# Input products of the mixers in another order, with attention and statistics woven between them

## The reference

```python
u = x @ w_in
u_conv, u_lru, q, k, v = jnp.split(u, [o1, o2, o3, o4], axis=-1)
y_conv = _conv_module(u_conv, conv_dw_w, conv_dw_b, conv_ln_g, conv_ln_b)
y_lru = _recurrent(u_lru, lru_conv_w, lru_conv_b, lru_wa, lru_ba, lru_wx, lru_bx, lru_lambda)
y_attn = _swa(q, k, v, band_bias, valid, sinks)
return jnp.concatenate([y_conv, y_lru, y_attn], axis=-1) @ w_out
```

## Time and profile before

| | |
|---|---|
| median of 3 runs | 3671.16 us (3669.0 to 3671.75) |
| the profiled execution | 3668.6 us, its span 3666.9 us |
| TensorE busy | 3374.3 us (92% of the span) |
| VectorE, ScalarE, GpSimd busy | 1614.5, 653.2, 310.9 us |
| stretch of mixer 0, first product to first output product | 465.4 to 652.2 us of the span |
| the same in mixer 1 | 1582.7 to 1772.2 us |

### The profile page before, as it was taken

The page is one execution under the profiler, slowest core; times in us unless marked ns, Lnnn a source line. Parts: engine busy times, 40 slices in busy tenths (PEclk is TensorE's granted clock), DMA queues, the critical chain, the costliest instruction groups (busy, mean ns, idle before and its releaser), DMA issues. The chain is left out here.

```text
span 3666.9 us, 38396 instructions
## 1 busy us (share of the span) xinstructions
PE 3374.3 (92%) x14592; PEld 2311.5 (63%) x14592; DVE 1614.5 (44%) x2304; ACT 653.2 (18%) x1051; POOL 310.9 (8%) x240
## 2 busy tenths in 40 slices
PE   6999995899998999986889998899969999899998
PEld 5888842488887888843478886745844443434342
DVE  4665355366636665446266644434334001311112
ACT  1111014211101111013221101422543000100001
POOL 2110000111101111000111101000320000100000
PEclk8999997999999999997999998899989999899999
DMA  5442220334323343221224421222112232799996
GB/s 135 108 124 80 80 62 19 81 86 114 95 89 87 91 114 94 80 58 35 81 66 106 109 86 48 69 69 81 35 45 71 72 100 93 306 409 410 410 407 240
DMA packets 490114, 453.18 MB, mean 124 GB/s; under 512 B 33994, under 2 KB 438781, under 8 KB 489756
## 3 DMA queue, kind: packets, MB, share of 16 engines
q1 hardware_dynamic: 487920, 449.97, 38.6%
q10 hardware_dynamic: 1452, 1.67, 0.4%
q0 software_dynamic: 640, 0.15, 0.0%
HBM read 445.96 MB, written 5.77 MB: 123 GB/s over the span
## 5 line engine op out<-in xcount | busy, mean ns | idle before, releaser
L454 PE MATMUL psum<-arena 128*128 128x256 f32 x7392 | 1621.6, 381 | 20.3 <-DVE arena L782 20.3
L454 PEld LDWEIGHTS psum<-arena 128*128 128x128 f32 x7392 | 1403.1, 190 | 221.4 <-issue 23.2
L847 DVE TENSOR_TENSOR arena<-arena 128x512 f32<-128x512 f32 (+2 forms) x152 | 96.5, 635 | 607.8 <-PE psum L454 578.8
L2118 PE MATMUL psum<-arena 128*64 128x512 f32 x1536 | 344.3, 598 | 0.8 <-ACT arena L2227 0.8
L351 POOL TENSOR_TENSOR arena<-arena 128x1024 f32<-128x1024 f32 x96 | 180.8, 1906 | 1045.8 <-DVE arena L837 1001.3
L2118 PEld LDWEIGHTS psum<-arena 128*64 128x64 f32 x1536 | 105.8, 136 | 231.9 <-issue 231.0
L678 ACT COPY arena<-psum 128x256 f32<-128x256 f32 x104 | 38.9, 374 | 1182.8 <-PE psum L454 1182.8
L1355 PE MATMUL psum<-arena 128*128 128x512 f32 (+1 forms) x576 | 216.8, 537 | 12.8 <-ACT arena L1571 6.5
L1547 PE MATMUL psum<-arena 128*128 128x512 f32 x512 | 220.3, 591 | 0.0
L2334 DVE SCALAR_TENSOR_TENSOR arena<-psum,arena 128x512 f32<-128x512 f32 x64 | 48.0, 751 | 330.4 <-PE psum L2128 330.1
L562 PE MATMUL psum<-arena 128*128 128x512 f32 x416 | 184.0, 603 | 9.8 <-DVE arena L991 6.3
(11 more groups left out here) (393 smaller groups left out, 2911.6 us busy)
## 6 DMA issues: line engine op xcount, KB each, us to landing
arena<-in_w_gate_dram SPq DMA_DIRECT2D x64, 1024.0 KB, 14.1
arena<-in_w_up_dram SPq DMA_DIRECT2D x64, 1024.0 KB, 14.6
arena<-in_w_down_dram SPq DMA_DIRECT2D x64, 1024.0 KB, 16.9
arena<-in_ffn_w_gate_dram SPq DMA_DIRECT2D x88, 512.0 KB, 5.6
arena<-in_ffn_w_up_dram SPq DMA_DIRECT2D x88, 512.0 KB, 7.2
arena<-in_ffn_w_down_dram SPq DMA_DIRECT2D x96, 384.0 KB, 3.8
arena<-in_w_in_dram SPq DMA_DIRECT2D x144, 256.0 KB, 3.2
arena<-in_ada_w_dram SPq DMA_DIRECT2D x48, 512.0 KB, 4.0
```

Of the source, the lines that this page charges most:

```text
L454: mm = pe.matmul(psum[:, b0 + b, c:c + HT], w, right(x), start=(first and c == 0), stop=last, skip_group_check=True)
L847: dve.tensor_tensor(sv[:, 0, :, :], a21, a22, ALU.add)
L2118: mm = pe.matmul(psum[64 * e:64 * e + 64, bank0 + half, :], x[:, k, 64 * e:64 * e + 64], ring[u % SLOTS][:, e, half * 512:(half + 1) * 512 ...
```

## The change

`MIX` is put in another order, and the work behind the 14 units is written between the last four of them, on all three engines:

```diff
-        MIX = [("a", 0), ("g", 0), ("a", 1), ("g", 1), ("xb", 0), ("xb", 1), ("gb", 0), ("gb", 1),
-               ("k", 0), ("v", 0), ("q", 0), ("q", 1), ("q", 2), ("q", 3)]
+        MIX = [("a", 0), ("g", 0), ("a", 1), ("g", 1), ("k", 0), ("v", 0), ("q", 0), ("q", 1),
+               ("q", 2), ("q", 3), ("xb", 0), ("xb", 1), ("gb", 0), ("gb", 1)]
```

```diff
+        prob += [arena[:, wsum_at:wsum_at + HEADS * 2 * WIN].rearrange("p (a b) -> p a b", b=2 * WIN),
+                 place(HEADS, 2 * WIN)]
```

TensorE (`unit(n)` is the old body of the loop over the units):

```diff
             def scores(l, n):
-                if n == 0:
+                if n:
+                    pe.wait_ge(s_used, l * 4 + n)
+                if n == 2:
                     pe.wait_ge(gates_ready, l + 1)
-                else:
-                    pe.wait_ge(s_used, l * 4 + n)
...
+                for n in range(10):
+                    unit(n)
+                pe.wait_ge(bank_free[0], l * 11 + 5)
+                pe.wait_ge(bank_free[1], l * 11 + 5)
+                scores(l, 0)
+                unit(10)
+
+                pe.wait_ge(conv_ready, l + 1)
+                for t in range(2):
+                    mm = pe.matmul(bank(2), ones256, conv[:, t, :], start=(t == 0), stop=(t == 1))
+                mm.then_inc(cmean_done, 1)
+                unit(11)
+                for t in range(2):
+                    pe.wait_ge(csq, l * 2 + t + 1)
+                    mm = pe.matmul(bank(3), ones256, conv_sq[:, t, :], start=(t == 0), stop=(t == 1))
+                mm.then_inc(cvar_done, 1)
+                scores(l, 1)
+                unit(12)
+
+                pe.wait_ge(s_used, l * 4 + 2)
                 pe.wait_ge(xc_ready, l + 1)
                 pe.wait_ge(gw_ready, l * 64 + 64)
                 for a in range(2):
...
                 mm.then_inc(gate_mm, 1)
...
+                unit(13)
+                scores(l, 2)
 
                 pe.wait_ge(bank_free[0], l * 11 + 7)
                 pe.wait_ge(bank_free[1], l * 11 + 7)
                 pe.wait_ge(cstd, l + 1)
-                scores(l, 0)
-                for n in range(4):
-                    if n < 3:
-                        scores(l, n + 1)
+                attend(l, 0)
+                scores(l, 3)
+                for n in range(1, 4):
                     attend(l, n)
```

ScalarE (`put(n)` empties the bank of unit n):

```diff
+                for n in (1, 3, 4, 5, 6, 7, 8, 9):
+                    put(n)
+                exps(l, 0)
+                for t in range(2):
+                    act.wait_ge(cdiff, l * 2 + t + 1)
+                    act.activation(conv_sq[:, t, :], conv[:, t, :], ACT.Square).then_inc(csq, 1)
+                act.wait_ge(cvar_done, l + 1)
+                act.activation(conv_rstd, bank(3), ACT.Sqrt, bias=eps_conv).then_inc(cstd, 1)
+                exps(l, 1)
                 act.wait_ge(gate_mm, l + 1)
...
                 last.then_inc(decay_ready, 1)
...
+                put(12)
+                put(13)
+                copies(l, 0)
+                exps(l, 2)
                 act.wait_ge(m2_ready, l + 1)
                 act.activation(mult, mult, ACT.Sqrt).then_inc(mult_ready, 1)
...
+                copies(l, 1)
                 for t in range(2):
                     act.wait_ge(cnorm, l * 2 + t + 1)
                     act.activation(yT[:, t, :], conv[:, t, :], ACT.Silu, bias=col(CBB + t))\
                        .then_inc(y_act, 1)
...
+                exps(l, 3)
+                copies(l, 2)
+                copies(l, 3)
```

More of the change, by code:

```diff
@@ L546, in mixer, with unit @@
             def mixer(l):
-                for n, (kind, _) in enumerate(MIX):
+                def unit(n):
+                    kind, _ = MIX[n]
                     side, g = n % 2, mix_at(l) + n
@@ L716, in mixer, with put @@
             def mixer(l):
[L717 to L720, removed]
+                def put(n):
+                    kind, t = MIX[n]
                     act.wait_ge(unit_done, mix_at(l) + n + 1)
@@ L982, in mixer, with recurrent_in @@
                 sink_of[0] = sinks[:, l * HEADS:(l + 1) * HEADS]
[L983 to L995, removed]
+                for t in range(2):
+                    dve.wait_ge(bank_free[1], l * 11 + t + 1)
+                    if t == 0:
+                        dve.memset(cpad[:, :, 0:30], 0.0)
+                        dve.memset(lpad[:, :, 0:3], 0.0)
+                    dve.tensor_tensor(cpad[:, t, 30:], sg[:, t, :], bank(0), ALU.mult)\
+                       .then_inc(bank_free[0], 1)
                 dve.drain()
-                taps(xc, lpad, 4, LW, LB).then_inc(xc_ready, 1)
                 taps(conv, cpad, 31, CW, CB).then_inc(conv_ready, 1)
-                dve.wait_ge(decay_ready, l + 1)
-                dve.tensor_tensor(i_gate, i_gate, xc, ALU.mult)
-                dve.tensor_tensor(r_gate, decay, decay, ALU.mult)
-                dve.drain()
-                dve.scalar_tensor_tensor(out=mult, in0=r_gate, scalar=1.0, in1=mult, op0=ALU.add,
-                                         op1=ALU.mult).then_inc(m2_ready, 1)
+                scores(l, 0)
+                def recurrent_in(t):
+                    n = 10 + t
+                    dve.wait_ge(unit_done, mix_at(l) + n + 1)
+                    dve.tensor_copy(lpad[:, t, 3:], bank(n % 2)).then_inc(bank_free[n % 2], 1)
+                recurrent_in(0)
                 dve.wait_ge(cmean_done, l + 1)
@@ L1009, in mixer @@
                        .then_inc(cdiff, 1)
-                dve.wait_ge(mult_ready, l + 1)
-                dve.tensor_tensor(i_gate, i_gate, mult, ALU.mult)
+                normalise(l, 0)
+                recurrent_in(1)
                 dve.drain()
-                for t in range(2):
-                    dve.tensor_tensor_scan(r_gate[:, t, :], decay[:, t, :], i_gate[:, t, :], 0.0,
-                                           ALU.mult, ALU.add)
+                taps(xc, lpad, 4, LW, LB).then_inc(xc_ready, 1)
+                scores(l, 1)
                 dve.wait_ge(cstd, l + 1)
@@ L1022, in mixer @@
                        .then_inc(cnorm, 1)
-                for t in range(2):
-                    dve.wait_ge(bank_free[t], l * 11 + 4)
+                normalise(l, 1)
+                dve.wait_ge(decay_ready, l + 1)
+                dve.tensor_tensor(i_gate, i_gate, xc, ALU.mult)
+                dve.tensor_tensor(r_gate, decay, decay, ALU.mult)
+                dve.drain()
+                dve.scalar_tensor_tensor(out=mult, in0=r_gate, scalar=1.0, in1=mult, op0=ALU.add,
+                                         op1=ALU.mult).then_inc(m2_ready, 1)
+                scores(l, 2)
+                scores(l, 3)
+                normalise(l, 2)
+                dve.wait_ge(mult_ready, l + 1)
+                dve.tensor_tensor(i_gate, i_gate, mult, ALU.mult)
+                dve.drain()
+                for t in range(2):
+                    dve.tensor_tensor_scan(r_gate[:, t, :], decay[:, t, :], i_gate[:, t, :], 0.0,
+                                           ALU.mult, ALU.add)
+                normalise(l, 3)
+                for t in range(2):
+                    dve.wait_ge(bank_free[t], l * 11 + 7)
                     dve.tensor_tensor(yT[:, 2 + t, :], r_gate[:, t, :], gelu_b[:, t, :], ALU.mult)\
                        .then_inc(y_dve, 1)
[L1028 to L1032, removed]
                 for i in range(KT):
```

29 lines of the change are left out of this document (6 added, 23 removed).

## The result

The changed kernel takes 3611.55 us (median of 4 runs, 3611.48 to 3612.3), the kernel before 3670.89 (3669.0 to 3671.75): 59.3 us less (1.6%), ratio 0.9839 with an interval of 0.9827 to 0.9852. The forecast was 3610. The profiled executions are 3612.3 and 3668.6, so by them the gain is 56.3, the difference of the spans too.

A forecast was written before the change was run, and what follows sets the result against it. The bound was the longest chain from the tenth unit to the first output product. It shortens by 30.5 us; with clock terms, 28.8 in mixer 0 and 32.1 in mixer 1, together 61: from 3671.2 to 3610, range 3603 to 3628.

The forecast's parts named there:

- Weaving shortens the chain from unit 9: Mixers, tenth unit to first output product: output products start at 621.7 instead of 652.22, 30.5 us less.
- The clock's term: TensorE in the attention: one product with v slowed by the lower clock per mixer, 1.7 us; bounds 0 to 9.
- The cover is 1.6 us, and each us beyond goes into the chain: VectorE's 31 taps and half the block 0 scores end at 547.5, before unit 10 ends at 549.1.
- Without them VectorE's scores of block 2 would wait: Without the added buffers, VectorE's scores of block 2 would wait for the transposes of block 0; no size given.
- ScalarE carries the chain from 573: Mixer 0: from block 1's exponentials (569.3 to 573.3), ScalarE carries the chain to the output products at 621.7.
- The signs of being wrong: Mixers: 31 taps run longer, a late unit takes twice its 6.9, or idle time precedes block 3's exponentials.
- Rival A: ScalarE's table loads: every switch drains it, 7 x 1.4 = 10 us per mixer, 3630; chance 0.08.
- Rival C: Output products wait for something else, such as weights; nothing gained, median stays at 3671; chance 0.03.
- Rival B: Short products between units drop TensorE's clock to its lower level, where it stays; 31 slower, 3702; chance 0.04.

The follow-up runs named there:

- The order alone: Kernel before with the input products in the new order and VectorE's 31 taps first, nothing woven; 3670.46 us beside 3671.74, ratio 0.9997.

## Why the prediction was right

- **Weaving shortens the chain from unit 9.** Right. Shifted by the 1.1 us by which mixer 0 of after is later in its span (its tenth unit ends at 541.34, in before at 540.2), the exponentials of block 1 were due at 570.4 and came at 570.40; the decay ended at 582.2 for 582.1; the exponentials of block 2 came at 591.32 for 591.1; the square root ended at 597.8 for 597.5. The prediction had left open by 0.7 whether ScalarE's copies of block 0 or VectorE's scores of block 2 end last ahead of these exponentials. In mixer 0 it was the copies, and it cost 0.2; in mixer 1 it was the scores, for which ScalarE waited 1.31.
- **The clock's term was too small.** From here the times slip: the exponentials of block 3 came at 609.27 for 607.4, the output products at 626.84 for 622.8, 4.0 late. The prediction had 1.7 for one slow product per mixer. In after two were slow, 3.68 and 3.74, and the transposes with them, 1.97. That is 2.3 and 2.0 in the two mixers, and with 0.3 outside them the 4.7 between 61.0 forecast and 56.3 in the profiles. That it is the clock is shown by the runs with spare products. They show too that the term was smaller than what the clock really takes: with both products at 2.04, mixer 0 was 5.8 shorter. Part of this was hidden in the prediction's other rows. Its 5.9 for the copies of block 1 and 11.1 for those of blocks 2 and 3 come from a stretch of before in which the transposes ran slow; in mixer 0 of the run with spare products the same copies took 5.1 and 10.2. These 1.7, the 1.7 of the sum and the 2.3 that it lacked make up nearly the 5.8.
- **The medians** came nearer than the mechanism did, 3611.6 for 3610, partly by luck: the profile of before lies 2.3 below its median, that of after 0.8 above.
- **"The cover is 1.6 us, and each us beyond goes into the chain"** was wrong. It looked at the first idle place of VectorE only; two more follow before its work is due. A pad of 3.45 cost nothing, one of 12.0 cost about 6.
- **"Without them VectorE's scores of block 2 would wait"** was right and of no weight: 0.61, and the chain did not get longer.
- **ScalarE carries the chain from 573.** Right, shown by the other order of its list, 9.6 per mixer.
- **The signs of being wrong** did not come: the 31 taps took 45.7 (46.0 forecast), a late unit 7.0, and no idle time stands ahead of the exponentials of block 3.
- **Rival A**, the drain at each switch, is excluded by the run with two more. **Rival C**: the output products start 0.2 behind the end of the last copy (626.64) in mixer 0, as before. The order alone, which was no rival in the prediction, is excluded too.
- **Rival B** did not come: TensorE's clock stayed at 1.00 through the late units, and the output products had it from 627 to 637. Two rows of before, mixer 0, show how the clock came back in the attention:

```profile
639.64 3.90 PE L531 MATMUL psum<-arena 128*128 128x128 f32 x16 [8.05 <-DVE arena L957]
644.22 2.04 PE L540 MATMUL psum<-arena 128*64 128x128 f32 x32 [0.68 <-ACT arena L710]
```

The 16 transposes behind 8.05 of idle time ran at a granted clock of 0.50, and the product with v right behind them at 1.00. Between the idle time and this product TensorE did nothing but transposes.

## What to carry to other kernels

When phases in which one engine works alone lie behind a dense stretch of another engine, split the dense stretch and put the first steps of the chain between its parts; a new order of the dense part was worth nothing by itself here. Then read the list of the engine that carries the chain: put its independent work into its waits. Here that was worth another 20 us, of which one table load less per mixer, 1.3 each by its row, is a small part. Slack has to be followed along an engine's whole list up to where its result is due, not to its next wait.

## What was not expected of the hardware

The same product with v of block 1 took 2.04 in mixer 0, where 2.27 us of idle time stood ahead of its transposes, and 3.74 in mixer 1, where it was 3.50. For block 2 it was 2.21 in both mixers, and the product took 2.04 and 3.74 again; so these rows do not give a rule for the length of one idle place. Products whose results nobody reads, put in such places, made one mixer 5.8 us shorter and the other 0.5. With ScalarE's list in the other order, 11 in place of 6 made both mixers 2.0 shorter, and the granted clock was 1.00 through the whole attention.
